# A two-block transformer kernel: the densest expert group's gate and up products as 512-column pairs

## The chip, the cores and the metric

The kernel runs on one core of a Trainium2 chip. The time is microseconds of device time for the whole program, from the fp32 inputs in HBM to the fp32 output in HBM. Three runs of the kernel before took 1722.1, 1722.77 and 1723.63 us; their median, 1722.77 us, is "the time before". One more execution was profiled; the rows below are its.

## The reference, cut to what matters

Two blocks of two layers each work on 256 tokens of width 1024. The second block (four SwiGLU feed-forwards of width 2816 and two mixers) isn't touched. The first block's two layers each end with a two-level mixture of experts, and the change lies there:

```python
def hier_moe(x, w_group, b_group, w_router, b_router, w_gate, w_up, w_down):
    probs_g = softmax(xf @ w_group + b_group)                 # 4 groups
    p_top, g_idx = lax.top_k(probs_g, 1)                      # one group for each token
    logits_e = (xf @ w_router + b_router).reshape(T, 4, 4)
    in_group = take_along_axis(logits_e, g_idx)               # 4 experts in the group
    w_top, e_local = lax.top_k(softmax(in_group), 2); w_top /= sum(w_top)
    gates = p_top * w_top, spread over the 16 experts         # two are nonzero for a token
    h = silu(x @ w_gate[e]) * (x @ w_up[e])                   # 1024 -> 256, for each expert e
    y = sum over e of (h * gates[:, e]) @ w_down[e]           # 256 -> 1024
```

## The kernel before, in words

**Products.** Every large product is fp32 made of three fp32r products. ScalarE copies an operand to its high part (`HI`, `HH`, `XTH`), VectorE subtracts that to get the low part (`LO`, `HL`, `XTL`), and TensorE adds high x high, high x low and low x high in PSUM (`split_product`, lines 388 to 391; the profile writes the moving operand first). Weights arrive as 1 MB units of 2048 columns by 128 partitions. SyncE loads them in the order in which they are used, into six slots in the expert stages (three of `RAW`, three of `AR`). `HI` and `LO` have three slots (`RING`); a slot is free when `w_used` tells that TensorE is done with its unit. A unit is split by `split()` in two halves of 1024 columns: ScalarE line 1189, VectorE line 1804.

**A mixture layer** (`moe` on each engine). VectorE's `router` finds each token's group and two experts from small products of TensorE, and ranks the four groups by their number of tokens. It first writes the order of the groups (`GI`, line 2094), from which SyncE takes the addresses of the expert weights (line 223) and issues the loads (line 187); then the selection matrix `SEL` (`sel_ready`, line 2114), and last the gates (`gt_ready`, line 2133). The largest group's four experts (c = 0 to 3) run densely on all 256 tokens. The other twelve run on gathered tokens: at most 128, 85 and 64 for the three groups. Line numbers of the stages:

- the gather, TensorE line 748: for each of eight k, two fp32 products of `XN` with `SEL` into one of three PSUM banks, 277 columns wide; ScalarE scales each to `XGF` (line 1383) and later copies and VectorE subtracts the parts for the groups (`gather_high`, line 1388, and `gather_low`). `slot_weights` is line 762: six tiny products that give the gate of each gathered slot. A transpose of the gates (line 755) goes to `gt_sb`, and GpSimd writes it to HBM and reads it back broadcast to `GB` (`gates`, lines 2694 and 2697).
- an expert of the largest group: `cols_T` twice. It keeps 128x128 of the weights stationary and moves 256 tokens, so gate and up are 2 x 48 products of 256 columns, and the hidden rows come out transposed. ScalarE applies silu (line 1396), VectorE multiplies by up (line 2148) and by the broadcast gates (`weigh`, line 2159), and the result is split to `HH` and `HL`. `rows` then gives 24 output products of 512 columns into `Y`.
- the order on TensorE: router products, in layer 0 also the other memory products that are left (`cols_half` and `cols_N`), in layer 1 fifteen idle products (`stay_awake(15)`, line 637), then the gather, line 762, experts 0, 1, rows of 0, expert 2, rows of 1, expert 3, rows of 2, expert 4 (gathered) and so on.

**The feed-forwards of the second block** already use another form, `pair`: it keeps 128x128 of the tokens stationary and moves 512 columns, 256 of gate and 256 of up, from two slots at once: 48 products of 512 columns. ScalarE splits the first halves of the next pair's units when `w_half` tells that this pair is half done (`first_halves`, line 1321), and after the pair's end it does two silus (line 1336) and the second halves (line 1327); VectorE follows (lines 1989 and 2004). The hidden rows must be transposed: four products of line 586, in the middle of `rows`.

## Time and profile before

| what | value |
|---|---|
| median of three runs | 1722.77 us |
| profiled execution | 1723.93 us, of which span 1722.2 us |
| TensorE busy | 1670.1 us, 97% of the span |
| VectorE, ScalarE busy | 1069.7 us (62%), 896.4 us (52%) |
| expert stages on TensorE | 192 to 388 us (layer 0), 543 to 740 us (layer 1) |

The profile gives each instruction's start, its duration and what ended the idle time before it. Matmuls overlap, so a duration is longer than the step from one start to the next; lengths of stages are taken here as differences of starts.

### The profile page before, as it was taken

The numbers are of one execution on the slowest core, as the hardware profiler recorded it, in microseconds if no ns is written. First come the engines' busy times: TensorE is split into PE (matmuls) and PEld (weight loads), VectorE is DVE, ScalarE is ACT, GpSimd is POOL, SyncE is SP. The second block draws the span as 40 slices with busy tenths as digits, with TensorE's granted clock in tenths as the row PEclk, the third lists the DMA queues.
The fourth block names the chain that finished last, engine by engine and source line by source line (L and its number), as shares of the span: only waits on it lengthen the run. The fifth ranks groups of instructions, "written<-read, shape, count | busy, mean of one in ns | idle before, by whom it ended". The sixth has DMA issues, their size and how long they took to land.

```text
span 1722.2 us, 24981 instructions
## 1 busy us (share of the span) xinstructions
PE 1670.1 (97%) x9821; PEld 1451.5 (84%) x9821; DVE 1069.7 (62%) x1410; ACT 896.4 (52%) x1273; POOL 82.1 (5%) x127
## 2 busy tenths in 40 slices
PE   8999999999989999999999999999999999999998
PEld 8998899878968998878887987888888888988886
DVE  7766577878556768875555466555555556665554
ACT  6555446765554457754445566444544445354443
POOL 8000020003000200000000000000000000000000
PEclk9999899999999999999999999999999999999999
DMA  8540767974304879755655334565555655545652
GB/s 265 158 147 25 237 217 251 339 265 156 115 1 152 273 234 334 269 174 171 196 188 169 114 111 163 177 197 186 179 174 192 190 175 171 191 161 176 205 180 89
DMA packets 236919, 317.13 MB, mean 184 GB/s; under 512 B 5609, under 2 KB 210752, under 8 KB 236832
## 3 DMA queue, kind: packets, MB, share of 16 engines
q1 hardware_dynamic: 234256, 309.09, 54.7%
q0 software_dynamic: 2576, 6.83, 1.5%
q8 instruction: 61, 1.00, 0.2%
q14 instruction: 26, 0.21, 0.0%
HBM read 314.84 MB, written 1.06 MB: 183 GB/s over the span
## 4 chain that ended last, share of the span: by engine, by line
PE 86%; DVE 7%; ACT 4%; issue 2%; DMA 1%; DVEq 0%; SPq 0%; ACTq 0%
PE PB L389 16%; PE PB L391 16%; PE PB L390 16%; PE Y L389 7%; PE Y L391 7%; PE Y L390 7%; PE PB L649 2%; DVE LO L1804 2%; PE PB L651 2%; PE PB L650 2%; ACT HI L1189 1%; PE Y L862 1%; PE PB L586 1%; PE PB L748 1%; DVE ST L1883 1%
## 5 line engine op out<-in xcount | busy, mean ns | idle before, releaser
L1804 DVE TENSOR_TENSOR LO<-RAW,HI 128x1024 fp32r<-128x1024 f32 (+3 forms) x322 | 375.4, 1211 | 135.4 <-ACT HI L1189 134.8
L1189 ACT ACTIVATE HI<-RAW 128x1024 fp32r<-128x1024 f32 (+3 forms) x322 | 313.3, 1024 | 78.0 <-PE Y L391 33.3
L389 PE MATMUL PB<-HI,XTH 128*128 128x512 f32 (+2 forms) x848 | 309.1, 365 | 2.2 <-DVE XTL L1853 1.5
L391 PE MATMUL PB<-HI,XTL 128*128 128x512 f32 (+2 forms) x848 | 307.8, 363 | 0.0
L390 PE MATMUL PB<-LO,XTH 128*128 128x512 f32 (+2 forms) x848 | 307.7, 363 | 0.0
L1989 DVE TENSOR_TENSOR LO<-RAW,HI 128x1024 fp32r<-128x1024 f32 x166 | 196.8, 1222 | 117.0 <-ACT HI L1321 97.9
L389 PE MATMUL PB<-XTH,HI 128*128 128x256 f32 x720 | 205.9, 286 | 5.2 <-DVE XTL L1824 2.2
L390 PE MATMUL PB<-XTL,HI 128*128 128x256 f32 x720 | 203.7, 283 | 0.0
L391 PE MATMUL PB<-XTH,LO 128*128 128x256 f32 x720 | 203.6, 283 | 0.0
L389 PEld LDWEIGHTS PB<-HI,XTH 128*128 128x128 f32 x848 | 160.0, 189 | 28.2 <-DVE XTL L1853 1.7
L391 PEld LDWEIGHTS PB<-HI,XTL 128*128 128x128 f32 x848 | 160.0, 189 | 25.0
L390 PEld LDWEIGHTS PB<-LO,XTH 128*128 128x128 f32 x848 | 160.0, 189 | 24.8
L389 PE MATMUL Y<-HI,HH 128*128 128x512 f32 x384 | 153.6, 400 | 1.1 <-DVE HL L1824 1.1
L391 PE MATMUL Y<-HI,HL 128*128 128x512 f32 x384 | 150.1, 391 | 0.0
L390 PE MATMUL Y<-LO,HH 128*128 128x512 f32 x384 | 149.8, 390 | 0.0
L389 PEld LDWEIGHTS PB<-XTH,HI 128*128 128x128 f32 x720 | 138.0, 192 | 7.7 <-DVE XTL L1824 2.6
L1321 ACT ACTIVATE HI<-RAW 128x1024 fp32r<-128x1024 f32 x83 | 84.0, 1051 | 110.2 <-PE PB L391 106.1
L390 PEld LDWEIGHTS PB<-XTL,HI 128*128 128x128 f32 x720 | 138.1, 192 | 0.4 <-issue 0.2
L391 PEld LDWEIGHTS PB<-XTH,LO 128*128 128x128 f32 x720 | 138.0, 192 | 0.0
L1804 DVE TENSOR_TENSOR LO<-AR,HI 128x1024 fp32r<-128x1024 f32 x96 | 121.0, 1310 | 1.6 <-ACT HI L1189 1.6
L1824 DVE TENSOR_TENSOR HL<-PB,HH 128x512 fp32r<-128x512 f32 (+3 forms) x64 | 36.1, 564 | 133.2 <-ACT HH L1341 93.8
L1189 ACT ACTIVATE HI<-AR 128x1024 fp32r<-128x1024 f32 x96 | 96.2, 1053 | 33.3 <-PE PB L391 23.0
(454 smaller groups left out, 2812.3 us busy)
## 6 DMA issues: line engine op xcount, KB each, us to landing
RAW<-in_ffn_pre_w_gate SPq DMA_DIRECT2D x22, 1024.0 KB, 5.4
RAW<-in_ffn_pre_w_up SPq DMA_DIRECT2D x22, 1024.0 KB, 7.3
RAW<-in_ffn_pre_w_down SPq DMA_DIRECT2D x22, 1024.0 KB, 4.9
RAW<-in_ffn_post_w_gate SPq DMA_DIRECT2D x22, 1024.0 KB, 5.4
RAW<-in_ffn_post_w_up SPq DMA_DIRECT2D x22, 1024.0 KB, 7.3
RAW<-in_ffn_post_w_down SPq DMA_DIRECT2D x22, 1024.0 KB, 4.9
AR<-in_w_gate SPq DMA_DIRECT2D x18, 1024.0 KB, 6.6
RAW<-in_w_down SPq DMA_DIRECT2D x18, 1024.0 KB, 5.5
```

The costliest lines, as they stand in the source:

```text
L389: pe.matmul(out_ap, ah, bh, start=start, stop=False)
L390: pe.matmul(out_ap, ah, bl, start=False, stop=False)
L391: return pe.matmul(out_ap, al, bh, start=False, stop=stop)
L586: mm = pe.transpose(PB[:, 2, j * S + t * P:j * S + (t + 1) * P], HT[:, t * UC + j * P:t * UC + (j + 1) * P], IDENT[:, :])
L649: pe.matmul(o, xh[:, k, :], HI[:, slot, w], start=k == 0, stop=False)
L650: pe.matmul(o, xh[:, k, :], LO[:, slot, w], start=False, stop=False)
L651: mm = pe.matmul(o, xl[:, k, :], HI[:, slot, w], start=False, stop=k == KC - 1)
L1189: act.activation(HI[:, slot, half], raw[:, half], ACT.Copy).then_inc(s["w_hi"], 1)
L1321: act.activation(HI[:, u % RING, 0:UNIT // 2], raw[:, 0:UNIT // 2], ACT.Copy).then_inc(s["w_hi"], 1)
L1804: ins = dve.tensor_tensor(LO[:, slot, c], raw_of(n.u)[0][:, c], HI[:, slot, c].bitcast(F32), ALU.subtract)
L1824: return dve.tensor_tensor(lo, src, hi.bitcast(F32), ALU.subtract)
L1989: ins = dve.tensor_tensor(LO[:, u % RING, c], raw_of(u)[0][:, c], HI[:, u % RING, c].bitcast(F32), ALU.subtract)
```

## The change

- SyncE loads the first expert's gate and up as four DMAs of half a unit: first halves of both, then second halves. The first halves count on `first_in`. ScalarE and VectorE split the two first halves before the second ones.
- `pair` becomes a function of its own, and the four dense experts use it: 48 products of 512 columns each, with four transposes for each expert. The gate of an expert is now a scalar for each token in VectorE's product, so the gate transpose, `gt_sb`, `GB`, `weigh` and GpSimd's `gates` go.
- The first pair stands ahead of the gather. The eight gathers stand one by one beside the rows of experts 0 and 1, four to each: the first ahead of the rows, the others at their quarters. They all use PSUM bank 3, so a gather waits until ScalarE has scaled the one before. `slot_weights` stands in the rows of expert 2.
- ScalarE scales the gathers after the second halves of the next pair. `gather_high` and `gather_low` of the groups move: group 1 to after expert 2, groups 2 and 3 to after expert 3 (before: at c = 1, 2 and 5).
- In layer 1 `stay_awake(15)` becomes `stay_awake(34)`. In layer 0 the claim of bank 0 goes from ahead of the gather to ahead of the second pair.

The diff, cut:

```diff
@@ SyncE, moe @@
                 read_order(range(1))
+                both = (a["w_gate"], a["w_up"])
+                for j in range(2):
+                    before_ = raw_of(n.u + j)[2]
+                    if before_ >= 0:
+                        sp.wait_ge(s["w_split"], before_ + 1)
+                for h in range(2):
+                    k = slice(h * KC // 2, (h + 1) * KC // 2)
+                    c = slice(h * (UNIT // 2), (h + 1) * (UNIT // 2))
+                    for j in range(2):
+                        raw, full, _, _ = raw_of(n.u + j)
+                        sp.dma_start(raw[:, c].rearrange("p (k n) -> p k n", n=UC),
+                                     both[j][layer, bass.ds(first[0], 1)].rearrange("e (k p) n -> p (e k) n", p=P)[:, k, :])\
+                            .then_inc(full if h else s["first_in"], 16)
+                n.u += 2
                 for c in range(EXPERTS + 1):
                     if c == 2:
                         read_order(range(1, 4))
-                    if c < EXPERTS:
+                    if 0 < c < EXPERTS:
                         expert(a["w_gate"], c, KC, UC)
                         expert(a["w_up"], c, KC, UC)
...
@@ TensorE: pair moves out of ffn @@
+            def pair(banks, spread, i=0, first=False, mid=None, new=False):
...
+                    pe.wait_ge(s["w_first"], n.next("wf") + i)
...
+                    if first or new:
+                        fresh(k)
...
@@ TensorE, moe @@
-                for b in range(4):
+                for b in range(0 if layer else 1, 4):
                     claim(b, counted=False)
                 if layer:
-                    stay_awake(15)
-                pe.wait_ge(s["sel_ready"], layer + 1)
+                    stay_awake(34)
                 x0 = KC * layer
 
-                def gather(ks):
-                    for k in ks:
-                        if k >= 3:
-                            pe.wait_ge(s["xg_f"], x0 + k - 2)
+                def gather(k):
+                    if k:
+                        pe.wait_ge(s["xg_f"], x0 + k)
+                    for t in range(NT):
+                        mm = pe.matmul(PB[:, 3, 0:SLOTS], XN[:, t, k * P:(k + 1) * P], SEL[:, t, :],
+                                       start=t == 0, stop=t == 1)
+                    mm.then_inc(s["xg_full"], 1)
+
+                def slot_weights():
+                    pe.wait_ge(s["gt_ready"], layer + 1)
+                    pe.wait_ge(s["xg_f"], x0 + KC)
...
-                gather(range(5))
-                pe.wait_ge(s["gt_ready"], layer + 1)
-                for t in range(NT):
-                    mm = pe.transpose(Y[0:4, 1, t * P:(t + 1) * P], SM[:, 64 + t * 16:68 + t * 16], IDENT[:, :])
-                mm.then_inc(s["rt_full"], 1)
-                gather(range(5, KC))
...
-                for c in range(EXPERTS + 1):
-                    if 0 < c <= 4:
-                        pe.wait_ge(s["h_mul"], n.next("hm"))
-                    if c < 4:
-                        claim(0)
-                        cols_T(0, new=c == 0)
-                        if c == 0:
-                            read(1)
-                        cols_T(1)
-                    elif c < EXPERTS:
...
+                spread = n.v % RING != 0
+
+                def turned(c):
+
+                    for j in range(2):
+                        for t in range(NT):
+                            mm = pe.transpose(PB[:, 1, j * S + t * P:j * S + (t + 1) * P],
+                                              HT[:, t * UC + j * P:t * UC + (j + 1) * P], IDENT[:, :])
+                    mm.then_inc(s["ht_full"], 1)
+
+                def first_turned():
+                    pe.wait_ge(s["first_h"], n.next("fh", 2))
+                    turned(0)
+
+                def next_turned(c):
+                    def middle(q):
+                        if q == 2:
+                            read(0)
+                            read(2)
+                            turned(c)
+                        if c < 3:
+                            gather(4 * c - 4 + q)
+                        elif q == 1:
+                            slot_weights()
+                    return middle
+
+                read(1)
+                read(3)
+                pair([PB[:, 1, :], PB[:, 3, :]], spread, new=True)
+                for c in range(1, 4):
+                    claim(0)
+                    claim(2)
+                    pair([PB[:, 0, :], PB[:, 2, :]], not spread, mid=first_turned if c == 1 else None)
+                    if c == 1:
+                        yclaim(0)
+                        yclaim(1)
+                        if layer == 0:
+                            pe.wait_ge(s["mk_done"], 1)
+                        pe.wait_ge(s["sel_ready"], layer + 1)
+                    pe.wait_ge(s["h_lo"], n.next("h"))
+                    if c < 3:
+                        gather(4 * c - 4)
+                    rows(HH, HL, 0, c == 1, False, quarter=next_turned(c))
+                n.next("wf")
+                for c in range(4, EXPERTS + 1):
+                    if c < EXPERTS:
+                        if c == 4:
+                            pe.wait_ge(s["gw_sb"], layer + 1)
                         if c in (4, 8, 12):
                             pe.wait_ge(s["xg_lo"], 3 * layer + c // 4)
 
@@ -781,8 +824,8 @@
 
                         claim(0)
                         gathered_cols(0, c // 4, mid if c > 4 else None)
+                        pe.wait_ge(s["h_lo"], n.next("h"))
                         if c > 4:
-                            pe.wait_ge(s["h_lo"], n.next("h"))
                             if c < 8:
                                 pe.wait_ge(s["st_ready"], n.at("st") + c - 4)
                         gathered_cols(1, c // 4)
...
-                    if c == 1:
-                        yclaim(0)
-                        yclaim(1)
-                        if layer == 0:
-                            pe.wait_ge(s["mk_done"], 1)
-                        pe.wait_ge(s["gt_sb"], layer + 1)
-                    if 0 < c <= 4:
-                        pe.wait_ge(s["h_lo"], n.next("h"))
-                        rows(HH, HL, 0, c == 1, False)
-                    elif c > 4:
-                        if c == 5:
-                            pe.wait_ge(s["gw_sb"], layer + 1)
+                    if c == 4:
+                        rows(HH, HL, 0, False, False)
+                    else:
                         gathered_rows(c - 1)
...
@@ ScalarE, moe @@
+                def dense(c):
+
+                    first_halves(1 if c == 0 else 2)
+                    n.v += 2
+                    act.wait_ge(s["w_used"], n.v)
+                    swapped = spread if c == 0 else not spread
+                    g = slice(UC, 2 * UC) if swapped else slice(0, UC)
+                    for t in range(NT):
+                        act.activation(SG[:, t * UC:(t + 1) * UC], PB[:, ((1, 3) if c == 0 else (0, 2))[t], g], ACT.Silu)\
+                            .then_inc(s["sg_done"], 1)
+                    second_halves(1 if c == 0 else 2)
+                    if c in (1, 2):
+                        gather_scaled(range(4 * c - 4, 4 * c))
+                    if c:
+                        used()
+                        hidden(c)
                     split()
+                    if c == 0:
+                        hidden(0)
...
+                act.wait_ge(s["first_in"], 16 + 32 * (layer + 1))
+                act.wait_ge(s["w_used"], n.u - RING + 2)
+                for u in range(n.u, n.u + 2):
+                    act.activation(HI[:, u % RING, 0:UNIT // 2], raw_of(u)[0][:, 0:UNIT // 2], ACT.Copy).then_inc(s["w_hi"], 1)
+                for u in range(n.u, n.u + 2):
+                    _, full, _, count = raw_of(u)
+                    act.wait_ge(full, 16 * count)
+                second_halves()
+                if layer == 0:
                     used()
                     act.activation(MV[:, 1, :, :], PB[:, 0, :], ACT.Copy).then_inc(p_free[0], 1)
-                gather_scaled(range(4))
-                split()
-                gather_scaled(range(4, KC))
-                split(2)
-                for c in range(EXPERTS):
+                split()
+                spread = n.v % RING != 0
+                for c in range(4):
+                    dense(c)
+                    for p in {2: (1,), 3: (2, 3)}.get(c, ()):
+                        gather_high(p)
+                for c in range(4, EXPERTS):
...
-                    if c in (1, 2):
-                        gather_high(c)
-                    if c == 5:
-                        gather_high(3)
...
@@ VectorE, moe @@
+                def dense(c):
+
+                    low(0, 1 if c == 0 else 2)
+                    n.v += 2
+                    swapped = spread if c == 0 else not spread
+                    up = slice(0, UC) if swapped else slice(UC, 2 * UC)
+                    if c == 0:
+                        dve.wait_ge(s["gt_ready"], layer + 1)
+                    for t in range(NT):
+                        dve.wait_ge(s["sg_done"], n.next("sg"))
+                        b, h = ((1, 3) if c == 0 else (0, 2))[t], slice(t * UC, (t + 1) * UC)
+                        dve.scalar_tensor_tensor(out=HT[:, h], in0=PB[:, b, up], scalar=SM[:, 64 + 16 * t + c:65 + 16 * t + c],
+                                                 in1=SG[:, h], op0=ALU.mult, op1=ALU.mult)\
+                            .then_inc(s["first_h"] if c == 0 else p_free[b], 1)
+                    low(1, 1 if c == 0 else 2)
+                    if c == 3:
+                        slot_gates()
+                    if c:
+                        used()
+                        hidden(c)
+                    split()
+                    if c == 0:
+                        hidden(0)
...
-                split()
-                slot_gates()
-                split(2)
-                for c in range(EXPERTS):
+                low(0)
+                low(1)
+                split()
+                spread = n.v % RING != 0
+                for c in range(4):
+                    dense(c)
+                    for p in {2: (1,), 3: (2, 3)}.get(c, ()):
+                        gather_low(p)
+                for c in range(4, EXPERTS):
                     used()
                     split()
-                    if c == 1:
-                        weigh(0)
-                        hidden(0)
                     product(c)
-                    if 0 < c < 4:
-                        weigh(c)
                     split()
...
@@ GpSimd @@
-            def gates(layer):
-
-                pool.wait_ge(s["gt_sb"], layer + 1)
-                pool.dma_start(gate_dram[layer], SM[0:4, 384:640]).then_inc(s["gt_out"], 16)
...
```

## Rows read from the trace of the kernel before

**Rows 1.** The page: busy time, share of the span and instructions of each engine
```profile
PE 1670.1 (97%) x9821; PEld 1451.5 (84%) x9821; DVE 1069.7 (62%) x1410; ACT 896.4 (52%) x1273; POOL 82.1 (5%) x127
```
**Rows 2.** Windows, layer 0: window, length, busy time by engine, PEclk, DMA share, GB/s
```profile
201.97:213.74 11.77, 11.77 (x98) 11.56 (x96) 7.29 (x9) 6.01 (x7) 1.09 (x2) 1.00 0.96 287
...
232.37:243.88 11.51, 11.51 (x97) 11.51 (x96) 11.51 (x8) 5.99 (x7) 7.06 (x4) 1.00 0.58 186
243.88:249.35 5.47, 5.47 (x26) 4.52 (x25) 4.31 (x5) 2.01 (x2) 0.00 (x0) 1.00 0.96 352
```
**Rows 3.** Timeline, TensorE, layer 0: start, duration, instruction, count, idle before and releaser
```profile
191.85 0.28 PE L391 MATMUL PB<-HI,CTL 128*128 128x256 f32 x1
192.82 4.94 PE L748 MATMUL PB<-AR,XN 128*128 128x277 f32 x20 [0.69 <-ACT MV L1425]
197.60 0.38 PE L755 MATMUL Y<-IDENT,SM 128*4 128x128 f32 x2
197.81 3.25 PE L748 MATMUL PB<-AR,XN 128*128 128x277 f32 x12
200.90 1.14 PE L762 MATMUL PB<-SM,AR 128*128 128x4 f32 x12
...
214.52 0.39 PE L389 MATMUL PB<-XTH,HI 128*128 128x256 f32 x1 [0.78 <-DVE HID L2148]
...
226.82 0.47 PE L389 MATMUL Y<-HI,HH 128*128 128x512 f32 x1 [0.53 <-DVE HL L1824]
```
**Rows 4.** Windows, first feed-forward: pair one, pair two, a later pair, its rows
```profile
753.25:764.26 11.01, 11.01 (x48) 8.90 (x48) 7.90 (x23) 7.25 (x11) 0.00 (x0) 1.00 0.45 130
765.12:776.60 11.48, 11.48 (x53) 9.48 (x53) 7.42 (x8) 5.68 (x7) 0.00 (x0) 1.00 0.61 209
...
782.53:793.41 10.88, 10.88 (x49) 9.01 (x48) 5.41 (x5) 4.50 (x5) 0.00 (x0) 1.00 0.83 271
793.41:799.32 5.91, 5.91 (x29) 4.90 (x28) 3.24 (x4) 2.73 (x4) 0.00 (x0) 1.00 0.18 38
```
**Rows 5.** Timeline, ScalarE, after the end at 793.41 of that later pair
```profile
793.61 0.84 ACT L1336 ACTIVATE HID<-PB,ST 128x256 f32<-128x256 f32 x2 [3.35 <-PE PB L391]
794.34 2.01 ACT L1327 ACTIVATE HI<-RAW 128x1024 fp32r<-128x1024 f32 x2
```
**Rows 6.** Timeline, VectorE, beside the second of those
```profile
795.43 2.36 DVE L1989 TENSOR_TENSOR LO<-RAW,HI 128x1024 fp32r<-128x1024 f32 x2 [0.43 <-ACT HI L1327]
```
**Rows 7.** Timeline, ScalarE, layer 1: the scaling of one gather
```profile
545.18 0.58 ACT L1383 ACTIVATE AR<-PB,PV 128x277 f32<-128x277 f32 x1 [0.35 <-PE PB L748]
```
**Rows 8.** Timeline, TensorE, layer 1, from the idle products to the first expert
```profile
538.32 3.67 PE L637 MATMUL PB<-CTH 128*128 128x512 f32 x15
543.00 4.94 PE L748 MATMUL PB<-AR,XN 128*128 128x277 f32 x20 [1.01 <-DVE AR L2114]
...
552.16 0.38 PE L389 MATMUL PB<-XTH,HI 128*128 128x256 f32 x1
```
**Rows 9.** Timeline, SyncE: the first expert load of layer 0 and of layer 1
```profile
182.81 0.40 SPq L187 DMA_DIRECT2D AR<-in_w_gate  x1
...
539.99 0.39 SPq L187 DMA_DIRECT2D AR<-in_w_gate  x1
```
**Rows 10.** DMA issues, those two: count, KB each, us from issue to landing
```profile
AR<-in_w_gate SPq DMA_DIRECT2D x1, 1024.0 KB, 5.6
...
AR<-in_w_gate SPq DMA_DIRECT2D x1, 1024.0 KB, 5.5
```
**Rows 11.** Timeline, layer 0, c = 6: ScalarE's copy of group 3, and TensorE's wait
```profile
288.89 0.62 ACT L1388 ACTIVATE XTH<-AR 128x512 fp32r<-128x512 f32 x1
...
290.63 0.39 PE L649 MATMUL PB<-HI,CTH 128*128 128x256 f32 x1 [0.49 <-DVE HL L1824]
```
**Rows 12.** Windows, for PEclk: layer 0's router, and a sparse stretch of layer 1
```profile
174.00:188.00 14.00, 14.00 (x74) 13.38 (x74) 9.73 (x54) 3.27 (x6) 0.00 (x0) 0.63 0.29 88
477.00:482.00 5.00, 2.52 (x16) 2.12 (x16) 4.03 (x8) 3.53 (x8) 0.00 (x0) 1.00 0.00 0
```

More of the change, by code:

```diff
@@ L551, in mem_outputs @@
                 mm.then_inc(s["ao_full"], 1)
+            def pair(banks, spread, i=0, first=False, mid=None, new=False):
+                if first:
+                    pe.wait_ge(s["w_split"], n.v + 2)
+                else:
+                    pe.wait_ge(s["w_first"], n.next("wf") + i)
+                    if mid is not None:
+                        pe.wait_ge(s["w_split"], n.v + 1)
+                slots = slice(0, RING, 2) if spread else slice(n.v % RING, n.v % RING + 2)
+                n.v += 2
+                for k in range(KC):
+                    if first or new:
+                        fresh(k)
+                    if k == KC // 2 and not first:
+                        pe.wait_ge(s["w_split"], n.v + i * RING)
+                        if mid is not None:
+                            mid()
+                    w = slice(k * UC, (k + 1) * UC)
+                    for t in range(NT):
+                        x = slice(t * P, (t + 1) * P)
+                        mm = split_product(banks[t], XTH[:, k, x], XTL[:, k, x], HI[:, slots, w], LO[:, slots, w],
+                                           k == 0, k == KC - 1)
+                    if k == KC // 2 - 1:
+                        mm.then_inc(s["w_half"], 1)
+                mm.then_inc(s["w_used"], 2)
@@ new lines, in slot_weights @@
+                def slot_weights():
+                    pe.wait_ge(s["gt_ready"], layer + 1)
+                    pe.wait_ge(s["xg_f"], x0 + KC)
+                    for p in range(1, 4):
+                        for t in range(NT):
+                            mm = pe.matmul(PB[0:CAPS[p], 3, 300 + 4 * p:304 + 4 * p], SEL[:, t, OFFS[p]:OFFS[p] + CAPS[p]],
+                                           F1[:, t, :], start=t == 0, stop=t == 1)
+                    mm.then_inc(s["gw_full"], 1)
+                spread = n.v % RING != 0
@@ L2054, in router @@
             def router(layer):
-                dve.wait_ge(s["rt_full"], 3 * layer + 1)
+                dve.wait_ge(s["rt_full"], 2 * layer + 1)
                 dve.wait_ge(s["rb_in"], 16 * 4)
@@ L2156, in weigh @@
-                def weigh(c):
-                    dve.wait_ge(s["gb_first" if c < 2 else "gb_in"], 16 * (layer + 1))
-                    ht = HT[:, :].rearrange("p (j t) -> p j t", j=2)
-                    dve.tensor_tensor(ht, ht, bc(GB[:, c, :].unsqueeze(1), 2, S), ALU.mult).then_inc(s["h_gb"], 1)
+                    dve.scalar_tensor_tensor(out=HT[0:cap, 0:UC], in0=SG[0:cap, 0:UC],
+                                             scalar=GW[0:cap, c // 4 - 1, c % 4:c % 4 + 1], in1=PB[0:cap, 1, 0:UC],
+                                             op0=ALU.mult, op1=ALU.mult).then_inc(s["h_mul"], 1)
@@ L2712, in _ @@
             norm(1, 21 + 48 + 1)
-            gates(1)
             norm(2, 21 + 48 + 14 + 4)
```

159 lines of the change are left out of this document (47 added, 112 removed).

## The prediction

> **What bounds the kernel now.** I read the page first: TensorE is busy for 97% of the span, the other engines for 62% and less [rows 1]. So a microsecond counts where TensorE's chain of work gets shorter, and nowhere else. Then I read the windows of the dense experts. TensorE is busy from end to end of each of them: 11.77 us for gate and up of the first expert, 11.51 us for those of a later one, 5.47 us for a set of rows, all at a granted clock of 1.00 [rows 2]. The timeline gives what stands between them: 0.69 us idle ahead of the gather, 0.78 us ahead of the second expert, 0.53 us ahead of the first rows [rows 3]. So the dense stage is a chain of TensorE instructions with 2 us of waits for each layer. What matters is how much TensorE work the change takes away, what it only moves, and which new waits it makes. For the new form the trace has a model, the feed-forward, which runs the same `pair` [rows 4 to 6].
>
> **The change, part by part.** All terms are for one layer unless told.
>
> Pairs. Before: 2 x 11.77 + 2 x 11.51 = 46.56 us (the second expert took as long as the first) [rows 2]. After: the first pair of the feed-forward took 11.01 us, the second, which holds the four transposes of the first hidden rows, 11.48, a later one 10.88 [rows 4]. 11.01 + 11.48 + 2 x 10.88 = 44.25 us, 2.3 us less. A 256-column product steps at 11.51 / 96 = 0.120 us and a 512-column one at 10.88 / 48 = 0.227, so doubling the width saves only 0.013 us on two products.
>
> Here a page speaks against the change. These rows give 0.6 us for a later expert. The Trainium skill (TensorE: Matmul & The Clock Gate, Back-to-back issue gap) gives N / 2.4 ns plus about 2.5 ns for N columns at full clock. By that, 96 products of 256 columns and 48 of 512 differ by 0.12 us, the eight pairs would save 1 us and not about 4.6, and the sum below would be some 3.6 us later. The trace has both forms at their own price, so I go by the rows.
>
> Rows and transposes. Three sets of rows (experts 0 to 2) get four transposes each (those of experts 1 to 3). A set without them took 5.47 us, one with them 5.91 [rows 2, 4]: 3 x 0.44 = 1.3 us more. (Expert 0's four are in the 11.48.)
>
> The two idle times of 0.78 and 0.53 us waited for the hidden rows of experts 0 and 1, which VectorE multiplied or split too late [rows 3]. Now the transposes stand half a pair or more behind the product. A pair's end to the end of its silus is 1.0 us in the feed-forward [rows 5], half a pair 5.4 us, so nothing waits: 1.3 us less. The gates as a scalar in VectorE's product, the removed `weigh`, and GpSimd's three DMAs cost TensorE nothing and give it nothing: they hid behind the pairs.
>
> The gather. Eight gathers took 200.90 - 192.82 less the gate transposes' 0.21, which go: 7.87 us, 0.96 each for the first five; line 762 took 201.97 - 200.90 = 1.07 us [rows 2, 3]. TensorE does one thing at a time, so "beside the rows" hides none of this; the 8.94 us are inserted in the dense stage. Taking them away from the front is counted below, with the start.
>
> The new wait. All gathers share bank 3, so the second of each four waits until ScalarE has scaled the first. ScalarE's order after a pair is two silus, both second halves (2.01 us), and only then the scaling. In the feed-forward the second halves end at 794.34 + 2.01 = 796.35, 2.94 us after the pair's end at 793.41 [rows 4, 5]. The scaling takes 0.58 us [rows 7], about 0.1 of it overlapped, and TensorE may go on at about +3.5 us. It arrives at one gather and one quarter of the rows, 0.96 + 5.47 / 4 = +2.33 us. So it idles for 1.17 us, at c = 1 and at c = 2: 2.3 us. At the third and fourth gather ScalarE has nothing else, and 0.58 us fits in a quarter of 1.37. The bounds: 0, if ScalarE were that much sooner, and 2 x 2.0 us, if the second halves waited for VectorE or a DMA too. I take 2.3, from the nearest rows. Queued behind ScalarE's scalings is the split of the next hidden rows, which are wanted only a whole pair later.
>
> Sum of the dense stage: -2.3 + 1.3 - 1.3 + 7.87 + 1.07 + 2.3 = +8.9 us for each layer.
>
> The start, layer 0. TensorE's last product ahead of the gather starts at 191.85 and it could go on at 191.97; the first expert starts at 201.97 [rows 2, 3]. The first pair needs the first halves of two units. Together they are 1 MB, like the first load, which is issued at 182.81 and lands 5.6 us later, at 188.4 [rows 9, 10]. ScalarE needs 2.0 us for two halves [rows 5], and VectorE ends 1.44 us behind it (797.79 against 796.35) [rows 5, 6]: 191.9. VectorE's router is over by then. The pair starts at about 192.0, with almost no slack: 10.0 us sooner. The copy of line 1425 no longer stands before anything, since the first pair uses banks 1 and 3. Net for layer 0: -10.0 + 8.9 = -1.1 us.
>
> The start, layer 1. Here no memory products cover the load. It is issued at 539.99 and lands at 545.5 [rows 9, 10]; plus 2.0 and 1.44 us and 0.1 for the semaphore, the pair starts at 549.1. Before, the gather filled the time from 543.00 on, and the first expert started at 552.16 [rows 8]. The gain is 3.1 us only: the gather stood in time that was empty anyway, and now it is paid elsewhere. The 34 idle products run to about 538.32 + 34 x 0.235 = 546.3 (15 took 3.5 us) and cost nothing, being over before the weights are; then TensorE idles for 2.8 us. The new wait `w_first` has only the pair behind it. Net for layer 1: -3.1 + 8.9 = +5.8 us.
>
> The gathered experts. ScalarE's copy of group 3 stood ahead of the hidden rows at c = 6, where TensorE idled for 0.49 us [rows 11]. It now stands ahead of c = 4, behind the split that the rows need; there the silu comes 1 us later, with 5 us to spare. I count 0.45 us less for each layer. The late loads need no more than before, since the stage before them got longer.
>
> **Sum:** -1.1 + 5.8 - 0.9 = +3.8 us. The profiled execution (1723.93 us, span 1722.2) becomes 1727.7. It stood 1.2 us above the median; on the median of 1722.77 the forecast is **1726.6 us**, 0.22% slower. What a measurement of this kernel can tell from no change is about 0.2%, 3.4 us, so the forecast lies at that border.
>
> **The rivals.**
>
> A, the clock falls in layer 1. In layer 0's router TensorE ran sparse small products, and the mean granted clock over 14 us was 0.63: 14 x 0.37 x 2 = 10.4 us at 1.2 GHz in place of 2.4 [rows 12]. After the change TensorE idles 2.8 us in layer 1, more than in any stretch after the start. For: that is new. Against: in a stretch of 5 us with only 2.5 busy the clock stayed at 1.00 [rows 12]. If it falls as in layer 0 and the idle time takes up some 3 us of the slow stretch, the pair loses half of the other 7: +3.5 us, 1730.1. The Trainium skill (TensorE: Matmul & The Clock Gate, Why this matters for your kernels) warns of idle gaps over about 3 us between bursts; this gap is just under that, so the rule is no verdict here.
>
> B, not slower: the shared bank doesn't stall. If ScalarE's scaling comes before TensorE arrives, because gathers and quarters between other instructions take 0.3 us longer each and the second halves are quick, the term of 2.3 us goes in both layers: 3.8 - 4.7 = -0.9, 1721.9 us. It decides at ScalarE's path under 2.3 us after the pair. The rows of the feed-forward say 3.5, so I give it little.
>
> C, the halves don't land sooner. If the engines work on all four DMAs at once, the first halves land with the second megabyte, 1.05 MB / 352 GB/s = 3.0 us later (rate from [rows 2]). Both starts slip by 3 us: +6, 1732.6. Against: in both layers the first load landed in 5.5 us [rows 10], though SyncE issues the next loads right behind it.
>
> D, faster: the start of layer 1 or the gathered stage gains over 7 us that I don't see. Nothing in the profile offers it; it stands for what I overlooked.
>
> **How the numbers follow.** Forecast (1724 to 1729) 0.60, A 0.13, C 0.07, B 0.12, D 0.08. The forecast's own range crosses the border of 1726.2: the stall's size and the landing can each take off 1 us. I count 0.30 of it as slower and 0.30 as the same. Slower: 0.30 + 0.13 + 0.07 = 0.50. The same: 0.30 + 0.12 = 0.42. Faster: 0.08. The range for 8 in 10 runs from B to above A: 1721 to 1731.
>
> **What would show it.** Right: pairs of 11.0, 11.5, 10.9 and 10.9 us; in each layer an idle time of about 1.2 us ahead of the second gather at c = 1 and c = 2, released by ScalarE; the first pair at 192 in layer 0, and in layer 1, about 1 us shifted, at 548, after 2.8 us of idle time; no wait at c = 6; layer 0's stage about 1.5 us shorter and layer 1's some 5 us longer. Wrong: a clock under 1.00 after 540 us (A), no idle time ahead of the second gathers (B), first halves landing 8 us after their issue (C), or pairs at a step other than 0.227 us.

## The result and the profile after

The change makes the kernel slower. Beside four runs of before (median 1722.43 us) the changed kernel took 1729.05, 1731.01, 1732.56 and 1733.48 us, median 1731.8: ratio 1.0048, 95% interval 1.0033 to 1.0063. Measured again beside 24 runs of before (1723.64), eleven runs had a median of 1729.11: ratio 1.0033, interval 1.0022 to 1.0044. So it costs 5.5 to 9.3 us; the forecast was 3.8. On the time before of 1722.77 us the two ratios make 1731.0 and 1728.5, the end of the forecast's range of 1721 to 1731 and inside it. The profiled execution took 1729.05 us with a span of 1727.3, 5.1 us above the span of before.

The page of the changed kernel, busy times as in [rows 1]:

```profile
PE 1672.9 (97%) x9484; PEld 1438.3 (83%) x9484; DVE 1055.4 (61%) x1408; ACT 896.8 (52%) x1281; POOL 78.3 (5%) x121
```

TensorE has 337 instructions fewer than before, yet 2.8 us more busy time; the other 2.3 us of the longer span are idle. Windows of layer 0, columns as in [rows 2]: pair one, pair two, rows with four gathers, pair three, rows with the slot weights. The last window is layer 1's first pair:

```profile
190.89:201.96 11.07, 11.07 (x49) 9.17 (x50) 5.95 (x5) 4.93 (x6) 0.00 (x0) 1.00 1.08 364
201.96:213.25 11.29, 11.29 (x54) 9.32 (x53) 7.42 (x8) 6.00 (x8) 0.00 (x0) 1.00 1.08 369
213.25:223.99 10.74, 9.92 (x45) 7.85 (x44) 6.14 (x4) 4.78 (x8) 10.28 (x4) 1.00 0.65 210
223.99:234.87 10.88, 10.88 (x49) 9.01 (x48) 5.42 (x5) 4.52 (x5) 2.21 (x3) 1.00 0.64 236
256.50:263.62 7.12, 7.12 (x42) 6.03 (x40) 3.44 (x7) 2.55 (x4) 0.00 (x0) 1.00 0.34 100
547.66:560.40 12.74, 12.74 (x49) 10.40 (x50) 5.95 (x5) 4.43 (x5) 0.00 (x0) 0.87 1.09 363
```

The pairs take what [rows 4] promised. A set of rows with four gathers took 10.74 us where a plain one took 5.47 [rows 2], with 0.82 us idle in it. The last line is the new thing: the same 48 products, 1.7 us longer, at a mean granted clock of 0.87.

ScalarE and TensorE in layer 0 after pair two (timelines; compare [rows 5] and [rows 7]):

```profile
213.44 0.66 ACT L1440 ACTIVATE HID<-PB 128x256 f32<-128x256 f32 x2 [2.99 <-PE PB L403]
213.99 1.06 ACT L1358 ACTIVATE HI<-RAW 128x1024 fp32r<-128x1024 f32 x1
214.94 1.06 ACT L1358 ACTIVATE HI<-AR 128x1024 fp32r<-128x1024 f32 x1
215.89 0.58 ACT L1417 ACTIVATE AR<-PB,PV 128x277 f32<-128x277 f32 x1
...
216.52 1.20 PE L758 MATMUL PB<-AR,XN 128*128 128x277 f32 x4 [0.82 <-ACT AR L1417]
```

Two silus, two second halves, then the scaling that the second gather needs: TensorE idles for 0.82 us, twice in each layer. (By starts each of these waits costs 1.09 us; see the experiment with two banks.)

Layer 1, timelines of SyncE, ScalarE, VectorE and TensorE (compare [rows 8] and [rows 9]):

```profile
538.06 0.39 SPq L239 DMA_DIRECT2D AR<-in_w_gate  x1
538.54 0.46 SPq L239 DMA_DIRECT2D AR<-in_w_up  x1
...
543.95 2.01 ACT L1477 ACTIVATE HI<-AR 128x1024 fp32r<-128x1024 f32 x2 [3.72 <-DMA AR<-in_w_up]
...
545.04 2.36 DVE L2038 TENSOR_TENSOR LO<-AR,HI 128x1024 fp32r<-128x1024 f32 x2 [1.63 <-ACT HI L1477]
...
536.33 8.01 PE L649 MATMUL PB<-CTH 128*128 128x512 f32 x34
547.66 0.47 PE L401 MATMUL PB<-HI,XTH 128*128 128x512 f32 x1 [3.32 <-DVE LO L2038]
...
548.66 0.43 PE L402 MATMUL PB<-LO,XTH 128*128 128x512 f32 x1
548.89 0.63 PE L403 MATMUL PB<-HI,XTL 128*128 128x512 f32 x1
```

TensorE does nothing for 3.32 us, while the weights land and are split. The 34 idle products stand in line 649. 1.2 us into the pair a product goes from 0.40 to 0.63 us: the granted clock fell from 2.4 to 1.2 GHz, for about 3.4 us.

To read all profiles alike I cut each at starts on TensorE. "Layer 0" runs from the first memory product behind the router (181.53 in before) to expert 4 (266.33), "attention" from the first product behind layer 0's experts (388.94) to layer 1's idle products, "layer 1" from there (538.32) to its expert 4 (616.53). The third column tells whether the clock was at its lower level in layer 0's router.

| kernel | median us | router of layer 0 | layer 0 | attention | layer 1 |
|---|---|---|---|---|---|
| before | 1722.8 | slow | 84.80 | 149.38 | 78.21 |
| before, again | 1723.7 | full | 83.09 | 149.35 | 78.20 |
| changed | 1731.8 | slow | 83.66 | 150.65 | 85.74 |
| changed, again | 1729.1 | slow | 83.24 | 151.68 | 83.33 |
| 46 idle products | 1730.4 | full | 85.81 | 150.67 | 84.10 |
| 15 idle products | 1729.8 | full | 85.96 | 153.98 | 86.37 |
| two banks | 1727.6 | full | 83.75 | 149.37 | 83.36 |
| whole loads | 1736.8 | slow | 85.34 | 152.80 | 87.28 |
| layer 1 gathers ahead | 1721.1 | slow | 83.68 | 155.22 | 75.85 |
| the same, two banks in layer 0 | 1717.6 | full | 81.69 | 151.59 | 75.84 |
| the same, again | 1716.3 | full | 83.71 | 149.34 | 75.85 |
| both layers ahead | 1716.5 | full | 83.79 | 151.83 | 75.86 |
| the same, again | 1718.2 | full | 81.48 | 151.78 | 75.85 |
| both ahead, whole loads | 1719.2 | slow | 81.67 | 152.00 | 76.11 |

The profiled difference of 5.1 us adds up from starts: up to the memory products -1.57 (the router's slow stretch was 6.8 us in place of 10.2), layer 0 -1.14, the gathered experts of layer 0 -0.55, attention +1.27, layer 1 +7.53, its gathered experts -0.04, the rest -0.41.

### The profile page after: what moved, and what is told of

Its sections match the earlier page's. It is cut to its first block, busy times and chain, and to the rows that moved or that the text cites. A ratio compares the mean times of both kernels' runs of the same rounds, so it can differ in the third digit from the quotient of the medians.

```text
span 1727.3 us, 24291 instructions
## 1 busy us (share of the span) xinstructions
PE 1672.9 (97%) x9484; PEld 1438.3 (83%) x9484; DVE 1055.4 (61%) x1408; ACT 896.8 (52%) x1281; POOL 78.3 (5%) x121
## 4 chain that ended last, share of the span: by engine, by line
PE 86%; DVE 7%; ACT 5%; issue 1%; DMA 1%; SPq 0%; DVEq 0%; ACTq 0%
PE PB L401 16%; PE PB L403 16%; PE PB L402 16%; PE Y L401 7%; PE Y L403 7%; PE Y L402 7%; PE PB L661 2%; PE PB L663 2%; PE PB L662 2%; DVE LO L1856 2%; PE Y L896 1%; PE PB L598 1%; ACT HI L1223 1%; PE PB L758 1%; DMA AR<-in_w_up 1%
## 5 line engine op out<-in xcount | busy, mean ns | idle before, releaser
L1856 DVE TENSOR_TENSOR LO<-RAW,HI 128x1024 fp32r<-128x1024 f32 (+2 forms) x306 | 356.3, 1210 | 116.5 <-ACT HI L1223 116.1
L401 PE MATMUL PB<-HI,XTH 128*128 128x512 f32 (+2 forms) x976 | 360.1, 369 | 6.0 <-DVE LO L2038 4.6
L403 PE MATMUL PB<-HI,XTL 128*128 128x512 f32 (+2 forms) x976 | 358.4, 367 | 0.0
L402 PE MATMUL PB<-LO,XTH 128*128 128x512 f32 (+2 forms) x976 | 358.1, 367 | 0.0
L1223 ACT ACTIVATE HI<-RAW 128x1024 fp32r<-128x1024 f32 (+2 forms) x306 | 297.3, 1023 | 63.1 <-PE Y L403 33.3
L1352 ACT ACTIVATE HI<-RAW 128x1024 fp32r<-128x1024 f32 x91 | 92.4, 1052 | 118.8 <-PE PB L403 114.5
L401 PE MATMUL PB<-XTH,HI 128*128 128x256 f32 x464 | 132.9, 286 | 4.0 <-DVE XTL L1876 2.2
L402 PE MATMUL PB<-XTL,HI 128*128 128x256 f32 x464 | 131.3, 283 | 0.0
L403 PE MATMUL PB<-XTH,LO 128*128 128x256 f32 x464 | 131.3, 283 | 0.0
L401 PEld LDWEIGHTS PB<-XTH,HI 128*128 128x128 f32 x464 | 89.0, 192 | 6.6 <-DVE XTL L1876 2.6
L1358 ACT ACTIVATE HI<-RAW 128x1024 fp32r<-128x1024 f32 x91 | 92.0, 1057 | 0.0
```

The costliest lines, as they stand in the source:

```text
L401: pe.matmul(out_ap, ah, bh, start=start, stop=False)
L402: pe.matmul(out_ap, ah, bl, start=False, stop=False)
L403: return pe.matmul(out_ap, al, bh, start=False, stop=stop)
L1223: act.activation(HI[:, slot, half], raw[:, half], ACT.Copy).then_inc(s["w_hi"], 1)
L1352: act.activation(HI[:, u % RING, 0:UNIT // 2], raw[:, 0:UNIT // 2], ACT.Copy).then_inc(s["w_hi"], 1)
L1358: act.activation(HI[:, u % RING, c], raw_of(u)[0][:, c], ACT.Copy).then_inc(s["w_hi"], 1)
```

## The experiments

My theory was that the gather had filled the time of the load in layer 1 and was taken out of it; that the shared bank adds four waits of 0.82 us; and that the idle time makes the clock fall. The rivals were that the place of the gather is indifferent, that the clock has another cause, and that the waits would be met elsewhere.

**The idle products, 46.**

```diff
-                    stay_awake(34)
+                    stay_awake(46)
```

> 46 idle products in layer 1 in place of 34, nothing else. Theory: the 3.3 us without work ahead of layer 1's first pair let TensorE's granted clock fall to 1.2 GHz, and with TensorE busy until the weights are there (46 x 0.235 = 10.8 us from 536.3, so to 547.2) it stays at 2.4. Then the clock is 1.00 after 540 us, the first pair takes 11.0 us and not 12.7, and the time is 1.7 us or more below the changed kernel's: 1728 to 1730, ratio to before 1.003 to 1.0045. Rival 1, the clock fell for another reason (the work around it, or chance): half clock again near 550 us, no gain, 1730 to 1733. Rival 2, the idle products delay the pair: it starts later than 547.7 and the time rises.

Measured: 1730.39 us, ratio 1.0040 (1.0027 to 1.0053). The idle time shrank and the first products kept the full clock (TensorE's timeline):

```profile
550.71 0.47 PE L401 MATMUL PB<-HI,XTH 128*128 128x512 f32 x1 [0.64 <-DVE LO L2038]
551.02 0.39 PE L402 MATMUL PB<-LO,XTH 128*128 128x512 f32 x1
551.25 0.40 PE L403 MATMUL PB<-HI,XTL 128*128 128x512 f32 x1
```

The pair was not delayed (11.37 us behind the first idle product, 11.33 before), and pair to expert 4 took 72.73 us in place of 74.41. So this profile agrees with the mechanism, but a second one of the changed kernel (further down) kept the full clock there with 34, and the time didn't move beyond the interval. This profile had a slow stretch in layer 0's first pair instead, after an idle time of 2.59 us.

**The idle products, 15.**

```diff
-                    stay_awake(34)
+                    stay_awake(15)
```

> The changed kernel with fifteen idle products in layer 1 as before the change, in place of 34; nothing else. They end 4.5 us sooner (19 x 0.235), so TensorE idles 7.8 us ahead of layer 1's first pair in place of 3.3. Theory: what TensorE does ahead of the pair sets the granted clock of the pair; with a longer idle time the half clock starts sooner or lasts longer, and the pair takes 12.7 to 16 us: 0 to 3.5 us above the changed kernel's 1731.8, and 2 to 5 us above the 1730.4 of 46 idle products. Rival, idle products have no bearing: the same time as 46 idle products gave, 1729 to 1731.

Measured: 1729.75 us, ratio 1.0035 (1.0022 to 1.0048). Layer 1's first product and the window of pair one:

```profile
552.17 0.76 PE L401 MATMUL PB<-HI,XTH 128*128 128x512 f32 x1 [7.60 <-DVE LO L2038]
```

```profile
552.17:565.00 12.83, 12.83 (x46) 10.39 (x47) 5.94 (x5) 4.44 (x5) 0.00 (x0) 0.81 1.09 361
```

The clock was already down when the pair began, and stayed so for 10.2 us, of which 5.3 lay in the idle time. Pair to expert 4 took 75.09 us, 2.4 more than at full clock. But 15, 34 and 46 idle products have medians of 1729.8, 1729.1 and 1730.4: a slow stretch is real and costs 1.7 to 2.4 us where it falls, and over many runs its prevention gave nothing measurable. The forecast of 2 to 5 us above 46 products was wrong.

**The gathers ahead in layer 1 alone.** The gathers of layer 1 go to three banks again, with fifteen idle products ahead of them, and ScalarE scales three of them ahead of its copies of the first halves and five behind:

```diff
-                        mm = pe.matmul(PB[:, 3, 0:SLOTS], XN[:, t, k * P:(k + 1) * P], SEL[:, t, :],
+                        mm = pe.matmul(PB[:, 1 + k % 3 if ahead else 3, 0:SLOTS], XN[:, t, k * P:(k + 1) * P], SEL[:, t, :],
...
+                if ahead:
+                    pe.wait_ge(s["sel_ready"], layer + 1)
+                    for k in range(KC):
+                        gather(k)
+                    pe.wait_ge(s["xg_f"], x0 + KC - 1)
```

> Layer 1 alone gathers ahead of the first pair again (three PSUM banks, fifteen idle products), with the load by halves and the pairs kept; layer 0 as changed. Theory: in layer 1 the change took the gather out of the shadow of the load, where it was free. Put back, 7.9 us of gathers and two waits of 0.82 us leave the dense stage, and the clock has no idle time to fall in (1.7 us or more); the pair starts 1 to 2 us later, since ScalarE scales most gathers only behind the first halves. In all 9.5 to 11 us below the changed kernel's 1731.8: 1720 to 1722.5, equal to before or a little below it. Rival, what counts is the new stage itself (pairs, transposes, order on ScalarE) and not where the gather stands: then the first pair starts as much later as the gathers take (7 to 8 us), and the time stays at 1729 to 1732.

Measured: 1721.09 us, ratio 0.9985 (0.9973 to 0.9997), 8 to 11 us below the changed kernel. The pair starts 12.73 us behind the idle products in place of 11.33 or 10.60, and layer 1 takes 75.85 us in place of 83.3 to 85.7. So what made the kernel slower is where the gathers of layer 1 stand, with the two waits that they meet there.

**Two banks.**

```diff
-                        mm = pe.matmul(PB[:, 3, 0:SLOTS], XN[:, t, k * P:(k + 1) * P], SEL[:, t, :],
+                        mm = pe.matmul(PB[:, 1 if k % 4 == 1 else 3, 0:SLOTS], XN[:, t, k * P:(k + 1) * P], SEL[:, t, :],
```

> The second gather of each four goes to PSUM bank 1 in place of bank 3, so that it needs no scaling of the first; the transposes wait until that gather is scaled. Theory: the four waits of 0.82 us go, 3.3 us, and the time is 1728 to 1729 (ratio 1.0033 or so); no idle time over 0.3 us ahead of the second and third gather. Rival, ScalarE's late scaling is met at the next step (the third gather, or the transposes, wait in place of the second): the 3.3 us stay or shrink by less than half, 1730.5 to 1732.

Measured: 1727.64 us, ratio 1.0029 (1.0019 to 1.0039). The rows of expert 0 with their four gathers, window and timeline:

```profile
214.39:224.04 9.65, 9.65 (x45) 7.93 (x44) 6.16 (x4) 4.78 (x8) 9.18 (x4) 1.00 0.45 146
```

```profile
214.39 1.10 PE L758 MATMUL PB<-AR,XN 128*128 128x277 f32 x4
216.69 1.10 PE L758 MATMUL PB<-AR,XN 128*128 128x277 f32 x4
219.43 1.10 PE L758 MATMUL PB<-AR,XN 128*128 128x277 f32 x4
```

9.65 us busy from end to end, 1.09 less than the 10.74 above, and no gather waits. A wait costs more than its idle time of 0.82 us: the second gather started 3.27 us behind the first and now starts 2.30 us behind it, and the rest of the 1.09 lies in the gather's own step (0.84 us against 0.73). From first pair to expert 4, with a slow stretch in the first pair, each layer took 72.2 us where forms with the waits took 74.3 to 74.4: 2.2 us for two waits, so they aren't met elsewhere. The median fell by 1.5 to 4.1 us where four waits make 4.4; the intervals of the ratios overlap, so the rows show it and the medians only agree.

**Whole loads.**

```diff
-                            .then_inc(full if h else s["first_in"], 16)
...
-                    if 0 < c < EXPERTS:
+                    if c < EXPERTS:
```

> The first expert's two units are loaded whole, gate first and then up, as before the change; everything else as changed. Theory: the first pair needs both units, so it waits for the second megabyte: in layer 1 the halves let it start at 547.7, whole units land some 2 us later and the pair starts at 549.5 to 550; in layer 0 the same, 193 in place of 190.9. The idle time of layer 1 grows to 5 us and the half clock stays. In all 3 to 4 us slower than the changed kernel, 1735 to 1736. Rival, loading by halves brings nothing, since the DMA engines work on all four transfers at once or the selection is what comes late: the same time, 1731 to 1733.

Measured: 1736.76 us, ratio 1.0072 (1.0056 to 1.0089). The first pair starts 12.63 us into layer 0 in place of 10.57 to 10.93, and 13.03 into layer 1 in place of 10.60 to 11.33; TensorE idles 5.01 us there. So in the changed kernel the halves save about 2 us in each layer. The medians differ by 5.0 to 7.7 us, more than the starts give and than I expected; these were four runs, at a mean granted clock of 0.9925.

**The gathers ahead in both layers.** The edit of layer 1 with `ahead` true in both.

> Both layers gather ahead of the first pair, in three banks; loads by halves and pairs kept. It tells whether moving the gather behind the first pair gained anything in layer 0, where memory products cover most of the load. Theory: in the profile of the changed kernel TensorE idled only 0.44 us ahead of layer 0's first pair, so the eight gathers (7.9 us) go nearly whole on the path there, while two waits of 0.82 us go: 6 us more than with layer 1 alone gathered ahead (1721.1), so 1726 to 1728. If the router of layer 0 runs at full clock, TensorE idles 2.6 us there (seen in two profiles), and the loss is 4 us: 1724.5 to 1726. Rival, the place of the gather is indifferent in layer 0: 1720 to 1722.

Measured: 1716.46 us, ratio 0.9953 (0.9935 to 0.9970) in five runs, at least 8 us below what I expected. My sum was wrong: I charged the gathers' 7.9 us ahead of the pair and forgot that they leave the rows. From first pair to expert 4 layer 0 then takes 63.12 us in place of 72.7. Run again beside the others:

> The kernel with all gathers ahead in both layers once more, beside the two-bank one, since its first five runs (1716.5) lay 8 us below what I had expected of it. The mistake of that expectation: the 7.9 us of gathers that come ahead of the pair leave the rows, so they cancel. By stages of its profile, layer 0 takes 63.1 us from first pair to expert 4 in place of 72.7, and 8.5 to 9.5 us more ahead of it. So layer 0 is 0 to 1.6 us shorter than in the changed kernel and layer 1 about 8 us shorter: 1718 to 1720. If 1716.5 was the true value, something else gains 2 us more.

Measured: 1718.23 us, ratio 0.9969 (0.9958 to 0.9979), as the corrected sum had it. Here TensorE waits in the gathers of layer 0, since ScalarE takes up the scalings only behind the halves:

```profile
187.55 2.97 PE L762 MATMUL PB<-AR,XN 128*128 128x277 f32 x12
192.53 4.94 PE L762 MATMUL PB<-AR,XN 128*128 128x277 f32 x20 [2.00 <-ACT AR L1428]
```

**Layer 1 ahead, and two banks in layer 0.** The gathers of layer 1 as in the third experiment, those of layer 0 as in the fourth.

> Layer 1 gathers ahead of the first pair, and in layer 0 the second gather of each four uses PSUM bank 1. The two gains should add, since they lie in different places: 1721.1 less the two waits of 0.82 us that are left in layer 0 gives 1719.5, ratio to before 0.9975, faster than before by about 4 us. Rival, the second bank's gain was chance or is met later: 1721.

Measured: 1717.60 us, ratio 0.9969 (0.9957 to 0.9981). And again:

> The kernel with layer 1 gathered ahead and two banks in layer 0, once more, for more runs beside the one with both layers gathered ahead. By stages it is 2.1 us shorter in layer 0 where the router ran at full clock in both profiles (81.7 against 83.8 us from the memory products to expert 4), and 0.7 where it did not. So it should be the fastest of all by 1 to 2 us: 1716 to 1718. Rival, the two can't be told apart.

Measured: 1716.26 us, ratio 0.9963 (0.9950 to 0.9977). Faster than before by 6.0 and 7.6 us. The medians lie 3.5 and 4.8 us under that of layer 1 alone, more than the 2.2 us of the two waits; the runs of layer 1 alone had a lower mean clock, too (0.9944 against 0.9951 and 0.9972). This one and the one with both layers ahead can't be told apart: 0.9969 and 0.9963 against 0.9953 and 0.9969. The 2.1 us in layer 0 that I expected between them was a slow stretch and not the form: with one ahead of or in the first pair the two forms took 83.71 and 83.79 us there, without one 81.69 and 81.48.

**Both ahead, whole loads.**

> As the kernel with all gathers ahead of the first pair in both layers, but the first expert's two units loaded whole, as before the change. It tells what loading by halves is worth once gathers cover the load. Theory: halves only help where the load is what the pair waits for. With the gathers ahead, TensorE is busy until 10.7 us after the start of the idle products (1.1 us of wait included), and whole units are split 13 us after it, where halves gave 12.7: 0 to 1.5 us slower for each layer, in all at most 3 us, so 1716.5 to 1719.5. Rival, the halves are what makes this kernel faster than before: with whole units it falls back to before's time or above, 1722 to 1725.

Measured: 1719.16 us, ratio 0.9974 (0.9964 to 0.9984). Layer 1 took 76.11 us where halves took 75.85. With gathers over the load, the halves are worth at most 0.3 us there (ScalarE's order differs a little, too: it scales four gathers and not three ahead of the first copies). Nearly all of the gain over before in layer 1 is then the pairs'.

**The changed kernel and the one before, again.**

> The changed kernel itself once more, beside the other three, for a second profile and more runs. Theory: work alone makes it 4.8 us longer (-1.1 in layer 0, +5.8 in layer 1 and so on) and a half clock in layer 1's first pair 1.7 us more; the rest of the difference is half clock in other places, which differs from run to run. So the idle time of 3.3 us and the half clock at the first pair of layer 1 are there again, and the median is 1729 to 1732, with a mean granted clock below that of before. Rival, the half clock at 549 us was chance: it is absent here, and the median is 1728 or less.

Measured: 1729.11 us, ratio 1.0033 (1.0022 to 1.0044). Half of the theory failed: the idle time was there (2.62 us), the slow stretch was not. First products and pair one of layer 1:

```profile
549.20 0.47 PE L401 MATMUL PB<-HI,XTH 128*128 128x512 f32 x1 [2.62 <-DVE LO L2038]
```

```profile
549.20:560.31 11.11, 11.11 (x49) 9.19 (x50) 5.95 (x5) 4.57 (x5) 0.00 (x0) 1.00 1.08 366
```

The pair started 8.87 us behind the first load's issue in place of 9.60. Even so layer 1 is 5.12 us longer than before.

> The kernel before itself, for a second profile of it. In eight of nine profiles with the change, TensorE's granted clock fell to 1.2 GHz somewhere in the attention of layer 1 (390 to 495 us), which took 1.2 to 5.8 us more than the 149.4 of the one profile of before. Theory: this is chance, and the kernel before meets it too; in a second profile its attention stage takes 149.4 to 155 us with a half-clock stretch, or its runs show mean clocks of 0.991 to 0.995 as often as those with the change. Rival, the change brings the fall on: the second profile of before shows no half clock there, and its runs lie higher in clock. The time against itself is 1.000.

Measured: 1723.68 us, ratio 1.0002 (0.9992 to 1.0011). The attention of layer 1 again ran at full clock (windows of before, before again, changed, changed again):

```profile
390.00:495.00 105.00, 95.74 (x694) 87.45 (x693) 71.90 (x102) 61.32 (x104) 13.92 (x6) 1.00 0.34 111
```

```profile
390.00:495.00 105.00, 96.21 (x705) 87.94 (x706) 71.02 (x101) 62.60 (x107) 13.93 (x6) 1.00 0.33 111
```

```profile
390.00:495.00 105.00, 95.39 (x688) 87.28 (x688) 70.01 (x100) 62.60 (x107) 13.92 (x6) 0.98 0.33 111
```

```profile
390.00:495.00 105.00, 96.16 (x682) 88.13 (x681) 68.72 (x99) 60.99 (x103) 13.42 (x6) 0.97 0.34 111
```

In the twelve profiles with the change or a form of it, ten show a slow stretch there, worth 1.3 to 5.8 us; in the two of before, none. The mean granted clock was 0.9949 over the eleven runs of the changed kernel and 0.9956 over the 24 of before beside them. A slow stretch of 3.4 us is 0.001 of the mean clock of a run (3.4 x 0.5 / 1724), so this difference neither shows one such stretch more in most runs nor excludes it. The kernel before meets further slow stretches as well, though no row shows where: 17 of its 83 runs had a clock of 0.994 or less, and its profile with a slow router had 0.996. Whether the change brings the falls in attention on stays open.

## Why the prediction was right or wrong

**The direction and the work were right.** From the changed kernel's profile, without what the clock did: layer 0 -1.14, gathered experts -0.55 and -0.04, layer 1 7.53 - 1.65 = +5.9, the rest -0.41. That is +3.7 us; the forecast's sum was +3.8. The sum is closer than its terms: by them the time from first pair to expert 4 is 44.25 + 3 x 5.91 + 7.87 + 1.07 + 2.3 = 73.2 us and it took 72.7, while in the first profile both starts came about 0.5 us later than forecast. These misses cancel, and that is luck. The 1.65 us is what the time from first pair to expert 4 grows by when a slow stretch falls in the pair (74.35 or so against 72.7 us).

**Pairs, transposes, idle times:** 11.07, 11.29, 10.88 and 10.88 us against 11.01, 11.48, 10.88 and 10.88 forecast. The old waits of 0.78 and 0.53 us are gone, and so is the one at c = 6: the stretch from expert 4 to the end of layer 0's experts is 0.46 to 0.55 us shorter.

**The gathers:** rows with four took 10.74 us; by the forecast's terms 5.47 + 3.93 + 0.44 + 1.17 = 11.0. The wait cost 1.09 us (10.74 against 9.65 with two banks) where the forecast had 1.17. TensorE arrived as forecast: unhindered, the second gather starts 2.30 us behind the pair (forecast 2.33). It went on at 3.27 us and not 3.5, since the silus took 0.66 us and not 0.84.

**The start:** the first pair stood at 190.89, 10.93 us behind the first memory product; forecast 192.0 - 181.53 = 10.5. In layer 1 it was 11.33 us behind the idle products; forecast 549.1 - 538.32 = 10.8, and in the second profile 10.60. The term that was short in the first profile is the landing: in layer 1 the second of the two first halves was issued 0.48 us behind the first and landed 5.4 us later, so both were there 5.9 us behind the first issue and not 5.5. In the second profile they were there 5.2 us behind it, so the landing varies by more than the miss.

**What was mis-sized is the clock.** The forecast put it at nothing. Rival A had it, at 0.13 and for one place. It happened at that place in the first profile (1.7 us) and not in the second. But the clock has three more places: layer 0's router, its first pair, and the attention of layer 1. The runs give it in sum: over the 72 runs of before that stand beside the experiments the time falls by 1.2 us for each 0.001 of mean granted clock, on a line through 1724.6 us at 0.9949. The changed kernel's eleven later runs had that clock and a mean of 1729.4: +4.8 us at equal clock. The first four had 0.9933 (rounded from 0.99325), where the line gives 1726.6, and a mean of 1731.5: +4.9 us. So about 5 us is the change's own at these clocks (an estimate; the changed kernel's eleven runs alone fall by only 0.75 us for each 0.001, so at a higher clock it is more), and what the first comparison shows above it goes with a lower clock in those four runs.

**One thing in layer 0 I did not ask.** I took the router's slow stretch of [rows 12] for a constant of the kernel. It isn't. Where the router ran at full clock, the memory products take some 1.7 us less, and before uses that at once (83.09 against 84.80 us). The changed kernel can't: its pair waits for the load. TensorE's idle time ahead of the pair, 0.44 us in the first profile and none in the second, was then 2.59 and 2.73 us, the clock fell in the pair, and layer 0 took 85.8 to 86.0 us. It is 1.1 to 1.6 us shorter than before's with a slow router and 2.8 longer with a full one. "With almost no slack", as I wrote, should have been a rival with a price.

Rivals B, C and D did not happen: the waits were there, the first halves landed 5.2 to 5.9 us after the first issue and not 8, and nothing came out faster.

At the end of layer 1's experts TensorE waited 2.41 and 2.35 us in the changed kernel's profiles against 1.41 in before: ScalarE's split of the next weights, ahead of the hidden rows in its queue, waited 2.13 us for their DMA against 1.12. I had counted the late loads at nothing; it is 1 us, and its cause wasn't followed up.

## What to carry over

Moving work "beside" other work of the same engine hides nothing; it only pays where the place that it leaves was not free. The gather filled a load's latency in layer 1, and the idle products put in its stead show that the place was empty. The wider products gave what the forecast said (2.3 us of the 2.4 by which layer 1 got shorter once the gather stood ahead), the earlier weights at most 0.3 us where the gather covers the load and about 2 us where nothing does. With the gather left ahead of the first pair, or only layer 0's moved and on two banks, the same pairs make the kernel 0.3 to 0.5% faster than before. When work moves, write both ends of it into the sum: I forgot the one end in one expectation and missed by 8 us. And read what a wait costs from starts: its idle time in the profile was a quarter short.

## What the runs showed of the hardware

TensorE's clock fell to 1.2 GHz around the first pair after idle times ahead of it of 2.59, 2.69, 2.72, 2.73, 3.21, 3.32, 5.01 and 7.60 us, and once at 2.61 us within the gathers; it stayed at 2.4 GHz after 0.44, 0.64, 1.84, 2.00, 2.29 and, once, 2.62 us. A slow stretch began up to 1.5 us after work had begun again or, after the two longest, in the idle time itself. The Trainium skill (TensorE: Matmul & The Clock Gate, Why this matters for your kernels) warns of gaps over about 3 us between bursts; here gaps of 2.59 to 2.73 us did it in five cases of six.

The same router of layer 0 ran at the lower clock in some executions and at the full one in others, with no change of the code: a profile of before took 1717.9 us of span without it and 1722.2 with it. Two kernels that differ by a few microseconds are therefore compared at equal mean clock, or over many runs.
